# HGRN sample steps: outer products over four row quadrants, new state as moving operand on four column tiles

## What is computed

```python
z = x @ w_in                       # columns: S5 input, q, f, i, out-gate, gate_a, gate_b
q = silu(q_pre); f = lb + (1 - lb) * sigmoid(f_pre); k = 1 - f; v = i_pre
S_t = diag(f_t) S_{t-1} + k_t v_t^T
o_t = S_t^T q_t
o = rms_norm(o, gain) * silu(g_pre)
```

## Time and profile before

| | us |
|---|---|
| median of 3 runs | 1558.46 (1557.3 to 1564.29) |
| span of the profiled execution, first to last instruction | 1552.5 |
| TensorE busy in the span | 1435.3 |
| DVE busy | 767.6 |
| ACT busy | 338.9 |
| mean granted clock of TensorE over the span | 0.949 |

### The profile page before, as it was taken

The page is one execution under the profiler, slowest core; times in us unless marked ns, Lnnn a source line. Parts: engine busy times, 40 slices in busy tenths (PEclk is TensorE's granted clock), DMA queues, the critical chain, the costliest instruction groups (busy, mean ns, idle before and its releaser), DMA issues.

```text
span 1552.5 us, 21337 instructions
## 1 busy us (share of the span) xinstructions
PE 1435.3 (92%) x8793; PEld 1086.3 (70%) x8793; DVE 767.6 (49%) x1504; ACT 338.9 (22%) x486; POOL 91.8 (6%) x96
## 2 busy tenths in 40 slices
PE   7988999999999999999999999989989889999672
PEld 6988998777778778878999996456555235656221
DVE  4787788888875236326566445321214222030328
ACT  4422331000010010015334335131012111111120
POOL 3820000000010100000010000100000000000000
PEclk9989999999999889979999999799999999999887
DMA  9434443333333443334564473699999999998992
GB/s 255 156 130 135 141 153 128 101 107 109 109 122 114 139 129 108 99 126 144 189 199 164 162 257 135 246 402 360 405 407 409 409 409 400 405 403 323 405 366 85
DMA packets 140543, 351.17 MB, mean 226 GB/s; under 512 B 20812, under 2 KB 21940, under 8 KB 140432
## 3 DMA queue, kind: packets, MB, share of 16 engines
q1 hardware_dynamic: 137320, 339.90, 60.2%
q0 software_dynamic: 3120, 9.84, 2.2%
HBM read 342.53 MB, written 7.18 MB: 225 GB/s over the span
## 4 chain that ended last, share of the span: by engine, by line
PE 82%; DMA 7%; DVE 6%; issue 2%; SPq 1%; ACT 1%; DVEq 0%; ACTq 0%
PE bank L534 80%; DMA mslot<-in_w_exp_up 4%; DMA mslot<-in_w_exp_down 3%; DVE atok L2459 1%; SPq L1218 1%; DMA raw<-in_w_in 1%; DVE ynorm L2585 0%; DVE lo L1659 0%; DVE stS L1987 0%; DVE ynorm L2590 0%; DVE stats L2540 0%; DVE ws L1834 0%; PE bank L928 0%; ACT hi L1369 0%; PE bank L817 0%
## 5 line engine op out<-in xcount | busy, mean ns | idle before, releaser
L534 PE MATMUL bank<-XT,raw 128*128 128x264 f32 x1280 | 311.2, 402 | 0.3 <-ACT GB L1458 0.3
L534 PEld LDWEIGHTS bank<-XT,raw 128*128 128x128 f32 x1280 | 249.8, 199 | 47.9 <-issue 4.6
L1659 DVE TENSOR_TENSOR lo<-raw,hi 128x2048 fp32r<-128x2048 f32 x68 | 162.1, 2385 | 120.9 <-ACT hi L1369 120.6
L1369 ACT ACTIVATE hi<-raw 128x2048 fp32r<-128x2048 f32 x67 | 128.2, 1914 | 215.7 <-PE bank L534 215.6
L534 PE MATMUL bank<-mslot,Xg 128*32 128x512 f32 (+1 forms) x1024 | 143.7, 649 | 28.7 <-DMA mslot<-in_w_exp_up 28.7
L534 PE MATMUL bank<-XH,hi 128*128 128x264 f32 x512 | 150.7, 294 | 4.9 <-DVE Q L2076 3.7
L534 PE MATMUL bank<-XL,hi 128*128 128x264 f32 x512 | 148.6, 290 | 0.0
L534 PE MATMUL bank<-XH,lo 128*128 128x264 f32 x512 | 147.9, 289 | 0.0
L534 PE MATMUL bank<-HT,mslot 128*128 128x264 f32 x512 | 116.6, 387 | 0.0
L534 PEld LDWEIGHTS bank<-mslot,Xg 128*32 128x32 f32 (+1 forms) x1024 | 38.3, 121 | 110.9 <-issue 110.2
L534 PEld LDWEIGHTS bank<-HT,mslot 128*128 128x128 f32 x512 | 96.5, 190 | 18.0 <-issue 1.7
(11 more groups left out here) (417 smaller groups left out, 2250.7 us busy)
## 6 DMA issues: line engine op xcount, KB each, us to landing
raw<-in_w_in SPq DMA_DIRECT2D x72, 1024.0 KB, 5.1
mslot<-in_w_exp_gate SPq DMA_DIRECT2D x128, 512.0 KB, 10.5
mslot<-in_w_exp_up SPq DMA_DIRECT2D x128, 512.0 KB, 11.7
mslot<-in_w_exp_down SPq DMA_DIRECT2D x60, 1024.0 KB, 14.4
raw<-in_w_out SPq DMA_DIRECT2D x16, 1024.0 KB, 5.0
mslot<-in_w_ple_gate SPq DMA_DIRECT2D x16, 1024.0 KB, 13.9
raw<-in_w_branch_b SPq DMA_DIRECT2D x8, 1024.0 KB, 5.0
raw<-in_w_branch_a SPq DMA_DIRECT2D x8, 1024.0 KB, 5.1
```

What stands on the lines that cost most here:

```text
L534: return nc.tensor.matmul(out, w, x, start=start, stop=stop)
L1369: nc.scalar.activation(hi[:, s % RH, :], raw[:, n % RD, :], ACT.Copy).then_inc(hi_done, 1)
L1659: v.tensor_tensor(lo[:, n % RD, :], raw[:, n % RD, :], hi[:, s % RH, :].bitcast(F32), ALU.subtract).then_inc(lo_done, 1)
```

## The change

The steps get names, `("outer", hh)`, `("sample", hh)`, `("turn", hh)`, `"mean"` and `"norm"`, and places of their own.

- **Outer products.** The samples' k and v are split into a high part and a low part in fp32r. ACT writes the high parts, DVE the low parts (`sample_lows`, at the end of its p = 0), each into two of four row quadrants of `skq` and `svq`, so that the quadrants hold the four pairs of high and low. `svblk` has 128 rows. One fp32r product per half of 512 columns, contracting over 128 rows, gives the sum of the four pairs. GpSimd sets `skq` and `svq` to zero once, ahead of the first state loads.
- **Sample products.** The new state is the moving operand (128 columns), and the weights are 32 columns of q, of which the last is the wanted one. Sample s goes to column tile s % 4, so that its o lands in row 31 of a quadrant, in a bank of its own ("os"). ACT copies it to `osam`; in the turn step, half a chunk later, TensorE transposes it twice, and ACT takes every 32nd column of the result and its square.
- **Places.** The outer product of head hh stands at 6.5 + 0.75 hh, its sample step half a chunk behind, its turn step another half chunk behind. The mean stands at 10.0 (before 9.75), the norm at 10.5 as before. The conversion of the GLU's input, which stood behind step 13 of the second half (at 9), stands behind its last turn step (9.75).
- **Mean and norm.** The mean's products have 32-column weights of ones on four column tiles; the norm's have one row of ones on four row tiles.
- **Banks.** From the first outer product of a half on, the ring has banks 4 and 5 too; at the start of the second half they are taken back, once read.
- The tables `colsel` and `rowsel` and one small load go.

```diff
-        steps = [0, 1, 1.75, 2.5, 3.25, 4, 4.75, 5.25, 5.75, 6.25, 6.75, 7.5, 8.25, 9, 9.75, 10.5]
+        steps = [(at_, p) for p, at_ in enumerate([0, 1, 1.75, 2.5, 3.25, 4, 4.75, 5.25, 5.75, 6.25])]
+        for hh in range(HG):
+            steps += [(6.5 + 0.75 * hh, ("outer", hh)), (7.0 + 0.75 * hh, ("sample", hh)),
+                      (7.5 + 0.75 * hh, ("turn", hh))]
+        steps += [(10.0, "mean"), (10.5, "norm")]
...
+                    if hg:
+                        ring[:] = [6, 7]
+                        for b in (4, 5):
+                            pe.wait_ge(misc_read[b], uses[b])
...
-                if 10 <= p <= 13:
-                    hh = p - 10
-                    stored(("sk", hg))
+                if what == "outer":
+                    if hh == 0:
+                        stored(("sk", hg))
+                        pe.wait_ge(h_scread, 16 * hg + 16)
+                        ring.extend([4, 5])
                     pe.wait_ge(h_blk, H0 + hh + 1)
                     for half in range(2):
                         b = side(("ou", hg, hh, half))
-                        mm(b[:, :], sktok[:, hh * 128:(hh + 1) * 128],
+                        mm(b[:, :], skq[:, hh * 128:(hh + 1) * 128],
                            svblk[:, half * 4:(half + 1) * 4, :].rearrange("p b v -> p (b v)"),
                            True, True).then_inc(misc_ready, 1)
...
-                    mm(b[:, 128:256], S0[:, hh, :], qt[:, 0, hh, 128:256], False, True)
+                    mm(b[:, 128:256], S0[:, hh, :], qt[:, 0, hh, 128:256], False, True).then_inc(misc_ready, 1)
+                    b = side(("os", hg, hh))
                     pe.wait_ge(h_new, H0 + hh + 1)
                     for s in range(NB):
-                        last = mm(b[:, T + s:T + s + 1], stS[:, hh % 2, s, :], Q[:, H0 + hh, T + s:T + s + 1],
-                                  True, True)
+                        rows = slice(32 * (s % 4), 32 * (s % 4) + 32)
+                        last = mm(b[rows, s // 4 * 128:(s // 4 + 1) * 128], Q[:, H0 + hh, T + s - 31:T + s + 1],
+                                  stS[:, hh % 2, s, :], True, True)
                     last.then_inc(misc_ready, 1)
-                if p == 14:
+                if what == "turn":
+                    stored(("os", hg, hh))
+                    b = side(("ot", hg, hh))
+                    for half in range(2):
+                        last = nc.tensor.transpose(b[:, half * 128:(half + 1) * 128],
+                                                   osam[:, hh % 2, half * 128:(half + 1) * 128], ident[:, :])
+                    last.then_inc(misc_ready, 1)
+                if p == "mean":
...
-                        last = mm(b[0:HG, 0:NT], colsel[:, hh, :], sq[:, hh, :], hh == 0, hh == HG - 1)
+                        last = mm(b[32 * hh:32 * hh + 32, 0:NT], ones[:, 0:32], sq[:, hh, :], True, True)
                     last.then_inc(misc_ready, 1)
-                if p == 15:
+                if p == "norm":
                     pe.wait_ge(h_rstd, hg + 1)
                     for hh in range(HG):
                         b = side(("rb", hg, hh))
-                        mm(b[:, 0:NT], rowsel[:, hh, :], rr[:, 1, :], True, True).then_inc(misc_ready, 1)
+                        mm(b[:, 0:NT], ones[32 * hh:32 * hh + 1, :], rr[32 * hh:32 * hh + 1, 1, :], True,
+                           True).then_inc(misc_ready, 1)
...
+            nc.gpsimd.memset(skq[:, :].bitcast(F32), 0.0).then_inc(h_zero, 1)
+            nc.gpsimd.memset(svq[:, :].bitcast(F32), 0.0).then_inc(h_zero, 1)
             for h in range(2):
                 pool.dma_start(stS[:, h % 2], state_view(t["state_hgrn"], h)).then_inc(h_stq[h % 2], 16)
...
+                    act.wait_ge(h_zero, 2)
+                    for name, dst, quads in (("sv", svq, (0, 64)), ("sk", skq, (0, 32))):
+                        b, read = side((name, hg))
+                        for r0 in quads:
+                            nc.scalar.activation(dst[r0:r0 + NB, :], b[0:NB, :], ACT.Copy).then_inc(h_kvh, 1)
...
+                if what == "turn":
+                    b, read = side(("ot", hg, hh))
+                    of_sample = b[:, 0:256].rearrange("p (s c) -> p s c", s=NB)[:, :, 31]
+                    nc.scalar.activation(O4[:, hh, T:NT], of_sample, ACT.Copy)
+                    nc.scalar.activation(sq[:, hh, T:NT], of_sample, ACT.Square).then_inc(read, 1)
...
+            def sample_lows(hg):
+
+                for n, (name, dst, quads) in enumerate((("sv", svq, (32, 96)), ("sk", skq, (64, 96)))):
+                    b, read = side((name, hg))
+                    dve.wait_ge(h_kvh, 4 * hg + 2 * n + 2)
+                    for r0 in quads:
+                        last = v.tensor_tensor(dst[r0:r0 + NB, :], b[0:NB, :], dst[0:NB, :].bitcast(F32),
+                                               ALU.subtract)
+                        if r0 == quads[0]:
+                            link(last)
+                    last.then_inc(read, 1)
+                settle()
...
-                    if (hg, p) == (1, 13):
+                    if (hg, p) == (1, ("turn", 3)):
```

More of the change, by code:

```diff
@@ L33 @@
 NST = 32
-HEADS = 8
+HEADS, HEAD = 8, 128
 HG = 4
@@ L71, in shape_constants @@
     c[:, C_MB:C_MB + 2] = (r[:, None] // 64) == np.arange(2)
-    for h in range(HG):
-        c[:, C_CS + h * HG + h] = 1.0 / 128
-        c[h, C_RS + h * 128:C_RS + (h + 1) * 128] = 1.0
+    c[:, C_MQ:C_MQ + 8] = (r[:, None] % 32) == np.arange(8)
     c[:, C_MASK:C_MASK + 128] = np.eye(128)
@@ L133, in build @@
     ones = const("ones", [P, 128])
[L134 to L138, removed]
+    small = const("small", [P, 16])
+    maskJ, maskC, maskB, maskQ = small[:, 0:4], small[:, 4:6], small[:, 6:8], small[:, 8:16]
+    router_at = used_const[0]
+    used_const[0] += 2048
     masks_at = used_const[0]
@@ L616, in hgrn @@
                         last.then_inc(misc_ready, 1)
-                if p <= 7:
+                if p in range(8):
                     if p:
@@ L1371, in hgrn @@
             def hgrn(hg, p):
+                what, hh = p if isinstance(p, tuple) else (p, None)
                 if p == 0:
-                    for n, name in enumerate((("v", hg, 0), ("v", hg, 1), ("sv", hg), ("sk", hg))):
-                        b, read = side(name)
-                        if n < 2:
-                            nc.scalar.activation(vtok[:, n].rearrange("p h v -> p (h v)"), b[:, :],
-                                                 ACT.Copy).then_inc(read, 1)
-                        else:
-                            nc.scalar.activation((svtok, sktok)[n - 2][:, :], b[0:NB, :], ACT.Copy).then_inc(
-                                read, 1)
+                    for c in range(2):
+                        b, read = side(("v", hg, c))
+                        nc.scalar.activation(vtok[:, c].rearrange("p h v -> p (h v)"), b[:, :],
+                                             ACT.Copy).then_inc(read, 1)
+                    act.wait_ge(h_zero, 2)
[3 more added lines that the diff above has]
+                            nc.scalar.activation(dst[r0:r0 + NB, :], b[0:NB, :], ACT.Copy).then_inc(h_kvh, 1)
                 if p == 8:
@@ L1389, in hgrn @@
                                          ACT.Copy).then_inc(read, 1)
-                if 11 <= p <= 14:
-                    hh = p - 11
+                if what == "sample":
                     b, read = side(("o", hg, hh))
-                    nc.scalar.activation(O4[:, hh, :], b[:, 0:NT], ACT.Copy)
-                    nc.scalar.activation(sq[:, hh, :], b[:, 0:NT], ACT.Square).then_inc(read, 1)
-                if p == 14:
+                    nc.scalar.activation(O4[:, hh, 0:T], b[:, 0:T], ACT.Copy)
+                    nc.scalar.activation(sq[:, hh, 0:T], b[:, 0:T], ACT.Square).then_inc(read, 1)
+                    b, read = side(("os", hg, hh))
+                    nc.scalar.activation(osam[:, hh % 2, :], b[:, 0:256], ACT.Copy).then_inc(read, 1)
+                if what == "turn":
[3 more added lines that the diff above has]
+                    nc.scalar.activation(sq[:, hh, T:NT], of_sample, ACT.Square).then_inc(read, 1)
+                if p == "mean":
                     act.wait_ge(h_ms, hg + 1)
@@ L1953, in hgrn @@
                     scores(hg, 0)
-                if 1 <= p <= 7:
+                    sample_lows(hg)
+                if p in range(1, 8):
                     if p < 7:
@@ L1998, in hgrn @@
                         spread(hg, hh + 1)
-                if p == 14:
+                if p == "mean":
                     b, read = side(("ms", hg))
-                    v.tensor_scalar(rr[:, 0, :], b[0:HG, 0:NT], RMS_EPS, None, ALU.add).then_inc(read, 1)
+                    v.tensor_scalar(rr[:, 0, :], b[:, 0:NT], 1.0 / HEAD, RMS_EPS, ALU.mult, ALU.add).then_inc(read, 1)
                     side_read(dve, ("ms", hg))
```

53 lines of the change are left out of this document (28 added, 25 removed).

## The result

The changed kernel takes **1495.77 us**, the median of 4 runs (1492.83 to 1499.68), beside 1560.24 (1557.3 to 1564.29) for the kernel before: a ratio of 0.9591 (0.9566 to 0.9617). The forecast was 1512.0 with a range of 1503 to 1530: right sign, 16 us too little, outside the range. The profiled execution took 1492.83, the shortest of the four, and its span is 1491.0; the span before was 1552.5, so 61.5 us are to be found.

The account below looks back on a forecast made before the run. TensorE's own queue, 92% busy, was taken as the bound. Gains 25.1 - 0.8 + 22.0 + 1.3 - 1.2 = 46.4 us bring the span from 1552.5 to 1506; with 6.0 around it, 1512, range 1503 to 1530.

Parts of the forecast that it names:

- so the whole shifts forward: Expert stage behind the change: its weight loads start behind TensorE, so everything there moves earlier with the gain kept.
- First half: First half of the heads, first outer product to norm step: 61.6 us becomes 36.5, a gain of 25.1.
- second half: Second half of the heads, first outer product to norm step: 59.4 us becomes 37.4, a gain of 22.0.
- Low parts and level 2: Behind the first half's norm: DVE's four low parts, 2.9 us, delay level 2; norm gain gone and 0.8 us lost.
- TensorE came for it at 587.95: Behind the first half's norm: TensorE took level 2's kt, ended at 585.84, 17.6 us behind the norm's start.
- End of the second half: Norm to the GLU chunks: 0.4 us gained at the first chunk and 0.87 at the second, 1.3 in all.
- A pause of 2 us at level 2 may cost one stretch at the lower clock: Level 2, behind the first half's norm: a TensorE pause may lower the clock once, 1.2 us off the gain.
- The 6.0 us around the span: Whole run: the median of 1558.46 lies 6.0 us above the profiled span of 1552.5, a difference taken to stay.
- A: Rival, chance 0.28: column tiles run one by one, or the clock still falls behind some sample steps; 1519 to 1531 us.
- B: Rival, inside the forecast's range: the state buffers' store and load become the bound; 1513 to 1518 us.
- C: Rival, chance 0.03: 32-column weights and transposes don't hold the clock, both halves at 1.2 GHz; 25 us slower, 1583.
- D: Rival, chance 0.04: DMA in the expert stage takes the gain back; 1550 to 1558 us.

Follow-up runs that it names:

- lows2: The changed kernel with DVE making its four low parts of the samples' v and k twice in each half; 1497.31 us, ratio 0.9613.
- samp_old: The changed kernel with the old sample products: new state as weights, one column of q moving, no turn step; 1502.27 us, ratio 0.9636.
- outer_old: The changed kernel with the old outer products: over 8 rows in plain f32, no low parts; 1510.15 us, ratio 0.9676.

## Why the prediction was wrong, and where it was right

**The main step that failed:** "so the whole shifts forward". I let all unchanged code behind the stage keep its length. The kernel before had a 20.5 us fall of the clock in the expert gather, and it goes away when the gather is moved: 9.6 us there, 8.6 of the 61.5 by the end of the span. That the change isn't needed for this is shown by b_pad9, the kernel before with 1.1 us of added work, which loses the fall and 7 us. My rows stopped at the stage; a stretch at 978 would have shown a clock of 0.50 with TensorE busy, and with it the risk. The 2.6 us ahead of the stage are falls of the clock too, but differ from execution to execution, and here they are luck. Together they are 11.2 of the 15.1 us by which the span (1491.0 against 1506.1) was missed. The chances had 0.05 for "better than the forecast", with no mechanism behind it.

**The stage**, 50.3 for 46.4:
- *First half* 25.1 forecast, 25.6 measured (28.2 at the norm step, less the 2.6); *second half* 22.0 and 22.35. The terms, forecast and then measured: outer products 0.46 and 0.65, sample products 0.76 and 0.57, mean 0.75 and 0.58, turn 0.22 and 0.22. The half chunk for the norm's scalars was right in kind: in the second half a wait of 0.91 for the reciprocal, forecast 0.9. The stretches came out at 38.0 and 39.0 us up to the norm step and not at "about 37", since the sum counted 120 records of w_in and the new places put 128 there. The clock's 22 us, for both halves together, were right too, against 1.00 after.
- *Low parts and level 2:* forecast a loss of 0.8, measured a gain of 1.3 (from the norm step to those 16 products 17.6 us before, 16.3 after). **The step "TensorE came for it at 587.95"** was wrong: the 16 products at that time take operands of level 1, done earlier; the row's `qt,kk` without `kt` says so, and lows2 shows it. The gain of the norm step itself remains (2.80 us before, 0.66 after), less a wait for k that was 0.34 and is 1.18 now:

```profile
548.68 0.60 PE L621 MATMUL bank<-ident,IV 128*8 128x128 f32 x4 [1.18 <-DVE kk L1986]
```

- *End of the second half:* 1.3 forecast, 1.1 measured. The 2.1 us that the norm step gains there are idle time ahead of the first GLU product (2.25), and what remains comes inside that product.
- *"A pause of 2 us at level 2 may cost one stretch at the lower clock":* there was no such pause; 1.2 taken off for nothing.
- *The 6.0 us around the span:* a run's time is 1.7 to 2.2 above its span in every result; by that, the profiled execution had been a fast one, which makes up the rest of the 6.0. For the medians it still holds roughly (1495.77 is 4.8 above 1491.0).

**The mechanism of the falls** was half right. That they go was forecast. The cause named, the products with one moving column, isn't enough (samp_old holds the clock with them); whether it has a part at the old places is open.

**Rivals.** *A:* the column tiles do overlap, and no fall came. *B:* the landing of stores held up GpSimd's queue in three cases, 11.5 us in all, and no engine waited for the state behind it. *C:* the clock is 1.00 in both halves. The Trainium skill, "TensorE: Matmul & The Clock Gate", Part 4, says that transposes don't count as busy for the clock in the way other products do; eight turn steps of two transposes have not lowered it, being 0.22 us each among large products, so the rule is neither borne out nor refuted by this trace. *D:* the end moved, and by more than the stage.

## What to carry to other kernels

Read the granted clock over the whole span, not only in the changed stretch: a long fall with a busy engine anywhere behind a change is time that a shift of a microsecond can give back or take, and the control for it is the old kernel with a microsecond of added work. If the clock falls behind small products, first try to put large products between them; here that took the falls out of the one execution traced (16.6 us of the stage) while the medians moved by 5.6, and once the forms were new it gave nothing. Compare single traces only with their runs' range beside them. And before a wait or a delay is priced, check by the operand names which step's result the row takes.

## What had not been expected of the hardware

- Four row tiles in the norm overlap: 8 records, 0.66 us, where eight records of 264 columns one by one would take 1.8 (an estimate from the 0.2225 us of a w_in record). The 16 sample records on four column tiles take 0.57.
- An 8-row f32 outer product seems to cost its neighbours time too: one head takes 9.11 us from outer to outer product in outer_old (515.87 to 524.98) and 7.45 in the changed kernel (518.83 to 526.28), 1.66 more, where the step alone is 1.26 longer.
- The lower clock can persist through work that holds the higher one: the same gather products run at 1.13 us a group in one position and stay at 2.08 for 20 us in another.
